# A two-layer transformer kernel: keys of the memory projected before the compression, weights loaded in 1 MB halves

## What is computed

```python
h = h + hier_moe(n2, ...)                                   # 32 experts, w1, w3, w2 of 2 MB each
gate = sigmoid(rms_norm(h, g_ple) @ w_ple_gate + b_ple_gate)
h = h + gate * (p @ w_ple_proj)
hn = rms_norm(h, norm_mix)
gq, gk, gv, gr, glr, nq, kc, vc, ks, vs, kw, vw, ng = split(hn @ w_in)
o_gla = gla_mixer(gq, gk, gv, gr, glr, ...)                 # decays by a running sum of log gates
o_nsa = nsa_mixer(nq, kc, vc, ...)                          # k_cmp = gelu(blocks(kc) @ w1) @ w2, the same for v
h = h + concat(o_gla, o_nsa) @ w_out
memn = rms_norm(mem, norm_mem)                              # 256 x 1024
k, v = memn @ wk, memn @ wv                                 # keys and values of the memory
h = h + cross_attn(rms_norm(h), k, v)
```

## Time and profile before

| what | us |
|---|---|
| median of 3 runs | 2139.96 (2139.68 to 2143.33) |
| the profiled execution, its own time | 2138.03 |
| its span, first to last instruction | 2136.3 |
| PE matmul busy | 1963.4 (92%) |
| DVE busy | 1377.9 (64%) |
| ACT busy | 1167.0 (55%) |
| HBM read | 415.36 MB, 195 GB/s over the span |

### The profile page before, as it was taken

The page is one execution under the profiler, slowest core; times in us unless marked ns, Lnnn a source line. Parts: engine busy times, 40 slices in busy tenths (PEclk is TensorE's granted clock), DMA queues, the critical chain, the costliest instruction groups (busy, mean ns, idle before and its releaser), DMA issues. The chain is left out here.

```text
span 2136.3 us, 29176 instructions
## 1 busy us (share of the span) xinstructions
PE 1963.4 (92%) x11497; PEld 1683.1 (79%) x11497; DVE 1377.9 (64%) x1828; ACT 1167.0 (55%) x1849; POOL 6.0 (0%) x27
## 2 busy tenths in 40 slices
PE   6998759999999998878889898999999999999997
PEld 5987448888888887367767577999999998888886
DVE  3552259999989898123543223999878896666665
ACT  3442149988989896124333242444477774545544
POOL 1000000000000000000000000000000000000000
PEclk9999869999999999989689999999999999999999
DMA  8433317999899899334012301455444444556664
GB/s 312 161 119 131 118 79 320 372 370 360 366 371 376 347 378 390 123 154 158 20 40 79 118 11 50 167 181 176 158 158 129 132 136 165 191 196 193 192 196 139
DMA packets 66175, 418.32 MB, mean 196 GB/s; under 512 B 12076, under 2 KB 14575, under 8 KB 49145
## 3 DMA queue, kind: packets, MB, share of 16 engines
q1 hardware_dynamic: 55728, 406.97, 51.3%
q10 hardware_dynamic: 10312, 9.48, 1.5%
HBM read 415.36 MB, written 1.06 MB: 195 GB/s over the span
## 5 line engine op out<-in xcount | busy, mean ns | idle before, releaser
L2113 DVE TENSOR_TENSOR slot_lo<-arena,w_hi 128x2048 fp32r<-128x2048 f32 x192 | 433.6, 2286 | 50.0 <-ACT w_hi L1579 49.9
L2468 DVE TENSOR_TENSOR tab_lo<-arena,tab_hi 128x1024 fp32r<-128x1024 f32 x256 | 312.4, 1224 | 122.9 <-ACT tab_hi L1884 120.8
L1579 ACT CAST w_hi<-arena 128x2048 fp32r<-128x2048 f32 x192 | 363.1, 1915 | 25.3 <-PE bank L1039 11.5
L1884 ACT CAST tab_hi<-arena 128x1024 fp32r<-128x1024 f32 x256 | 267.6, 1046 | 0.2
L1435 PE MATMUL bank<-x_hi,tab_lo 128*128 128x256 f32 x1024 | 145.0, 285 | 7.9 <-DVE tab_lo L2468 7.9
L1435 PE MATMUL bank<-x_hi,tab_hi 128*128 128x256 f32 x1024 | 148.5, 288 | 2.0 <-ACT tab_hi L1884 2.0
L1035 PE MATMUL bank<-w_hi,gathP 128*128 128x512 f32 x512 | 142.5, 401 | 7.6 <-ACT gathP L1584 5.4
L1918 ACT CAST e_hi<-arena 128x256 fp32r<-128x256 f32 x128 | 52.0, 407 | 175.1 <-PE bank L1468 174.4
L1435 PE MATMUL bank<-nT_lo,tab_hi 128*128 128x256 f32 x1024 | 143.0, 281 | 0.0
L1039 PE MATMUL bank<-slot_lo,gathP 128*128 128x512 f32 x512 | 140.3, 396 | 0.5 <-DVE slot_lo L2113 0.5
L1891 ACT ACTIVATE arena<-bank 128x256 f32<-128x256 f32 (+16 forms) x128 | 43.9, 343 | 175.1 <-PE bank L1435 175.0
(11 more groups left out here) (407 smaller groups left out, 3240.5 us busy)
## 6 DMA issues: line engine op xcount, KB each, us to landing
arena<-in_w_dram SPq DMA_DIRECT2D x96, 2048.0 KB, 12.0
arena<-in_peer_down_dram SPq DMA_DIRECT2D x128, 512.0 KB, 3.3
arena<-in_peer_up_dram SPq DMA_DIRECT2D x128, 512.0 KB, 4.3
arena<-in_packed_later_dram SPq DMA_DIRECT2D x18, 2048.0 KB, 7.8
arena<-in_packed_first_dram SPq DMA_DIRECT2D x14, 2048.0 KB, 8.7
arena<-in_packed_later_dram SPq DMA_DIRECT2D x1, 1632.0 KB, 15.7
arena<-in_packed_later_dram SPq DMA_DIRECT2D x1, 1536.0 KB, 12.3
h<-in_x_dram ACTq DMA_DIRECT2D x1, 1024.0 KB, 4.9
```

The costliest lines, as they stand in the source:

```text
L1579: nc.scalar.copy(hi_of(e, g), portion_of(slot, e, g)).then_inc(S("w_hi"), 1)
L1884: nc.scalar.copy(tab_hi[n % HI][:, :], tab[n % PR]).then_inc(S("table_hi"), 1)
L2113: nc.vector.tensor_tensor(portion_of(slot_lo, e, g), portion_of(slot, e, g), hi_of(e, g).bitcast(F32), ALU.subtract).then_inc(S("w_lo"), 1)
L2468: nc.vector.tensor_tensor(tab_lo[n % PR][:, :], tab[n % PR], tab_hi[n % HI][:, :].bitcast(F32), ALU.subtract).then_inc(S("table_lo"), 1)
```

## The change

The parts are these.
- Loads: every slot is loaded by two DMAs of 1 MB (column halves) with a semaphore each. In the expert stage a half is loaded when its own portion is used up, and ACT's cast of a portion waits for its half alone; `w2` is laid out anew so that its halves are column halves too. Elsewhere both halves wait for the same event as before, and users wait for both. PEER's table loads keep their size and use the slot semaphores.
- Between the layers: ACT reads gate tiles 0 and 1, squares the memory (`mem_sq`), casts the two portions, reads gate tile 2, does the first half's norm statistics, reads gate tile 3, does the second half's. PE sums the memory's squares behind the gate tiles; DVE normalises the memory behind `norm_cols`.
- Projection: the logarithm and running sum stand beside the fourth to sixth portion; the positions are turned behind `glr`; `dup` stands ahead of `nq`. The phase ends behind the projection and behind the compression are gone; DVE starts its GLA preparation when `nq` is done.
- The eight key tiles stand behind `nq`, whole, in banks 4 to 7. Then `gla_far`, the hidden layer of the compression, `gla_near`, the compression's outputs, `gla_blocks`, the output products, the compressed scores, the transposes.
- The sparse loop: only the eight value tiles are left, half a tile (8 matmul instructions) in each of steps 3 to 18.
- Two extra semaphores of the router are folded into others.

```diff
-    for name in ("w1", "w3", "w2"):
+    for name in ("w1", "w3"):
         arrays[name] = np.stack([rows_on_partitions(e) for e in inputs[name][0]])
+    arrays["w2"] = np.stack([np.concatenate([rows_on_partitions(e[:, 512 * x:512 * x + 512]) for x in range(2)], axis=1)
+                             for e in inputs["w2"][0]])
     arrays["peer_down_2"] = inputs["peer_down_2"].reshape(NKEYS, P, KT, P).transpose(0, 3, 2, 1).reshape(NKEYS, P, D)
...
-            if g < 4:
-                return v[:, 2048 * (g % 2):2048 * (g % 2) + 2048].rearrange("p (k n) -> p k n", n=512)
-            return v[:, :].rearrange("p (k n) -> p k n", n=D)[:, :, 512 * (g % 2):512 * (g % 2) + 512]
+            return v[:, 2048 * (g % 2):2048 * (g % 2) + 2048].rearrange("p (k n) -> p k n", n=512)
...
-        mem_sq = scratch(B0, KT, T)
-        xkT = scratch(B0, KT, T)
+        mem_sq = scratch(B0 + 4608, KT, T)
+        xkT = small[:, :].rearrange("p (k t) -> p k t", t=T)
...
-        landed = [S(f"slot_landed_{r}") for r in range(RING)]
+        landed = [[S(f"landed_{r}_{x}") for x in range(2)] for r in range(RING)]
...
+            for x in range(2):
+                half_ready(eng, n, x, i)
+
+        def half_ready(eng, n, x, i=0):
+
+            eng.wait_ge(landed[n % RING][x], i * 16 + 16 * (n // RING + 1))
...
+            b = tile_bank(pe, ("mem_sums", 0))
+            pe.wait_ge(S("mem_squared"), 1)
+            for k in range(KT):
+                mm = nc.tensor.matmul(b[:, 0:T], lhsT=ones[:, :], rhs=mem_sq[:, k, :], start=k == 0, stop=k == KT - 1)
+            mm.then_inc(S("tile_done"), 1)
...
-            for b, m in ((0, 0), (1, 1), (4, 2), (5, 3)):
+
+            pe.wait_ge(S("pos_ready"), 1)
+            pe.wait_ge(S("tile_read"), tile_no["kv", 3] + 1)
+            for m in range(4):
                 for g in range(2):
...
-                    mm = nc.tensor.matmul(bank[b][:, T * g:T * g + T], lhsT=sel_dup[:, g, :], rhs=kvT[:, m, :],
+                    mm = nc.tensor.matmul(bank[m][:, T * g:T * g + T], lhsT=sel_dup[:, g, :], rhs=kvT[:, m, :],
                                           start=True, stop=True)
                 mm.then_inc(S("dup_done"), 1)
...
+            layer_T(pe, "mix2", "nq", ports[6:8], 0)
...
+            def mem_part(c, b, ks):
+                at = LATE_AT + 9 + c // 4
+                slot_ready(pe, at)
+                wv = slot_view(at, KT, 512)
+                for k in ks:
+                    if c < KT:
+                        lhsT, rhs = wv[:, k, P * (c % 4):P * (c % 4) + P], memT[:, k, :]
+                    else:
+                        t, x = c % 4 // 2, c % 2
+                        lhsT, rhs = memT[:, k, P * t:P * t + P], wv[:, k, T * x:T * x + T]
+                    mm = nc.tensor.matmul(b[:, 0:T], lhsT=lhsT, rhs=rhs, start=k == 0, stop=k == KT - 1)
+                if ks[-1] == KT - 1:
+                    mm.then_inc(S("tile_done"), 1)
+                    if c % 4 == 3:
+                        spent(at)
+
+            pe.wait_ge(S("mem_normed"), 1)
+            for c in range(KT):
+                mem_part(c, tile_bank(pe, ("mem", c)), range(KT))
...
+            pe.wait_ge(S("cmp_in_ready"), 2)
             gla_far()
+            cmp_hidden()
             gla_near()
+            cmp_out()
             gla_blocks(1)
             gla_blocks(2)
             pe.wait_ge(S("gla_far_copied"), 2)
...
                 mm.then_inc(S("gla_out"), 1)
+            cmp_score()
...
+            def value_half(c, half):
+                if half == 0:
+                    n = tile_no["mem", c] = len(tile_no)
+                    if c >= KT + 2:
+                        pe.wait_ge(S("tile_read"), n - 1)
+                mem_part(c, bank[6 + c % 2], range(4 * half, 4 * half + 4))
...
-                if 0 <= i - MEM_FROM < MEM_TILES:
-                    mem_tile(i - MEM_FROM)
+                if 0 <= i - MEM_FROM < MEM_HALVES:
+                    value_half(KT + (i - MEM_FROM) // 2, (i - MEM_FROM) % 2)
...
-                slot_ready(act, MOE_AT + 3 * e + g // 2)
+                half_ready(act, MOE_AT + 3 * e + g // 2, g % 2)
...
+            gate(0, 0)
+            gate(0, 1)
+            act.wait_ge(S("mem_in"), 16)
+            nc.scalar.activation(mem_sq[:, :, :], memT[:, :, :], ACT.Square).then_inc(S("mem_squared"), 1)
             layer_first(act, "mix2")
-            norm_act(act, chain, "mix2", h, ple_added)
+            gate(1, 0)
+            norm_act_rows(act, chain, "mix2", h, 0, ple_added)
+            gate(1, 1)
+            norm_act_rows(act, chain, "mix2", h, 1, ple_added)
+            b = tile_in(act, ("mem_sums", 0))
+            nc.scalar.activation(mem_rms, b[:, 0:T], ACT.Sqrt, bias=eps[:, 0:1], scale=1.0 / D).then_inc(S("tile_read"), 1)
+            act.wait_ge(S("tile_read"), tile_no["mem_sums", 0] + 1)
+            act.sem_inc(S("mem_rooted"), 1)
...
+                if q == 2:
+                    act.wait_ge(S("tile_read"), tile_no[("loga", 1)] + 1)
+                    chain(nc.scalar.activation(log_tmp, loga[:, :, :], ACT.Abs))
+                    chain(nc.scalar.activation(log_tmp, log_tmp, ACT.Exp, scale=-1.0))
+                    nc.scalar.activation(log_tmp, log_tmp, ACT.Ln, bias=1.0).then_inc(S("log_part"), 1)
+                if q == 6:
+                    act.wait_ge(S("dup_done"), 4)
+                    for s in range(2):
+                        nc.scalar.copy(dupT[:, 2 * s:2 * s + 2, :].rearrange("p g t -> p (g t)"), bank[2 + s][:, :])
...
-            act.wait_ge(S("cmp_w1_in"), 32)
-            phase_end(act, "act")
...
-            nc.scalar.copy(posT[:, :, :].rearrange("p s i -> p (s i)"), bank[6][:, 0:2 * SUB]).then_inc(S("pos_ready"), 1)
             k_exp(0)
-            act.wait_ge(S("dup_done"), 4)
-            for s in range(2):
-                nc.scalar.copy(dupT[:, 2 * s:2 * s + 2, :].rearrange("p g t -> p (g t)"), bank[4 + s][:, :])
+            read_mem(0)
             act.wait_ge(S("diag_diff"), 1)
             nc.scalar.activation(diag[:, :, :, :], diag[:, :, :, :], ACT.Exp).then_inc(S("diag_exp"), 1)
+            read_mem(1)
             q_exp(1)
             k_exp(1)
+            read_mem(2)
             q_exp(2)
+            for c in range(3, KT):
+                read_mem(c)
             act.wait_ge(S("cmp_hidden"), 1)
-            nc.scalar.activation(cmp_h[:, :, :], bank[2][:, 0:64].rearrange("p (s n) -> p s n", s=2)[:, :, 0:2 * N_CMP],
...
+
+            dve.wait_ge(S("mem_rooted"), 1)
+            chain(nc.vector.reciprocal(mem_rms, mem_rms))
+            for k in range(KT):
+                ins = nc.vector.scalar_tensor_tensor(out=memT[:, k, :], in0=memT[:, k, :], scalar=col("norm_mem_2", k),
+                                                     in1=mem_rms, op0=ALU.mult, op1=ALU.mult)
+            ins.then_inc(S("mem_normed"), 1)
+
+            def decays(q, x):
+                if (q, x) != (3, 0):
+                    return
+                dve.wait_ge(S("log_part"), 1)
+                chain(nc.vector.tensor_scalar(loga[:, :, :], loga[:, :, :], 0.0, None, ALU.min))
+                chain(nc.vector.tensor_tensor(loga[:, :, :], loga[:, :, :], log_tmp, ALU.subtract))
+                chain(nc.vector.tensor_scalar(loga[:, :, :], loga[:, :, :], 0.5 / 16.0, None, ALU.mult))
+                for c in range(2):
+                    ins = nc.vector.tensor_tensor_scan(bcum[:, c, :], loga[:, c, :], loga[:, c, :], 0.0, ALU.add, ALU.add)
+                chain(ins)
+                cg = nsa_gate[:, 0, :].rearrange("p (a b) -> p a b", b=3)[:, :, 0]
+                nc.vector.tensor_scalar(cg, cg, late_row[:, 0:1], None, ALU.mult)
+
+            layer_dve(dve, "mix2", ("glr", 0), decays)
+            dve.wait_ge(S("tile_done"), tile_no["nq", 3] + 1)
 
...
+                width = src.shape[1] // 2
+                for x in range(2):
+                    if n >= RING:
+                        m = n - RING
+                        if m in spent_at:
+                            sp.wait_ge(S("tile_done"), spent_at[m])
+                        else:
+                            e, kind = (m - MOE_AT) // 3, (m - MOE_AT) % 3
+                            wait_portion(sp, e, 2 * kind + x)
+                    cols = slice(width * x, width * x + width)
+                    sp.dma_start(slot[n % RING][:, cols], src[:, cols]).then_inc(landed[n % RING][x], 16)
...
+                    for x in range(2):
+                        if j % 3 < 2:
+                            sp.wait_ge(S("w13_used"), i * 8 + (4 * (j // 3 - 2) + 2 * (j % 3) + x + 1))
+                        else:
+                            sp.wait_ge(S("w2_used"), i * 4 + (2 * (j // 3 - 2) + x + 1))
+                        cols = slice(2048 * x, 2048 * x + 2048)
+                        sp.dma_start(slot[(MOE_AT + j) % RING][:, cols], src[:, cols]).then_inc(
+                            landed[(MOE_AT + j) % RING][x], 16)
             for m, pieces in enumerate(later):
```

(30 more changed lines are left out.)

197 lines of the change are left out of this document (70 added, 127 removed).

## The result

The changed kernel takes 2086.30 us (median of 4 runs, 2085.36 to 2090.44) against 2140.34 of the kernel before on the same chip: ratio 0.9749, 95% interval 0.9732 to 0.9766, a gain of 54.0 us where 45.3 were forecast. 2086.3 lies inside the range of 2079 to 2111. The profiled execution took 2087.17 us, 50.9 less than the one of before (2138.03).

The account below looks back on a forecast made before the run. PE was taken as the bound, busy in 92% of 2136.3 us. Terms -7.2 - 2.0 + 3.5 + 4.3 - 10.4 - 27.5 - 6.0 = -45.3 us took 2139.96 to 2094.7; range 2079 to 2111.

Parts of the forecast that it names:

- step 3: End of `nq` to the loop: key tiles fill PE's wait, thin matmuls lose the clock; 73.4 us against 69.1, +4.3 us.
- Between the layers: Last gate tile to projection: casts and first-half statistics hide under gate products, projection starts at 911.8; -7.2 us.
- The clock's share: Projection's start: with less idle time ahead it need not begin at the lower clock; -2 us, between 0 and -2.1.
- `dup`: Projection: its 16 instructions, moved ahead of `nq`, take 3.44 us at full clock; +3.5 us.
- Start of the loop: Loop's start to first memory tile: about 7 us remain of 17.4; -10.4 us.
- The loop: Sparse loop: eight of 16 tiles leave it while PE stays the bound; -27.5 us, second-half steps 4.66 us.
- The rival of a loop bound by its chain: Sparse loop: steps can't go under perhaps 4.8 us because of DVE and ACT stages; +13 us, 2107.7; chance 0.15.
- Halves in the expert stage: Expert stage: ACT's 8.4 us of weight waits should go, most having reached PE; -6 us, between 0 and -8.4.
- the one with full clock behind the keys: Hidden layer through output products: PE's idle time drops the clock, so it stays full; 13.2 us more gain, 2081.5; chance 0.17.
- The stage bound by DMA: Expert stage: 8 KB rows move only at 377 GB/s, an expert takes 19.2 us instead of 17.0; 2170.7; chance 0.04.

Follow-up runs that it names:

- e5_order_back: The changed kernel with ACT's order between the layers put back, casts and both gates ahead of the row statistics; 2099.81 us.
- e9_spread_late: The changed kernel with the hidden layer's 64 thin products behind the last four key tiles, sixteen behind each; 2082.94 us.
- e11_bare_loop: The changed kernel with all 16 value halves in step 0 of the sparse loop and none later; 2100.78 us.
- e3_both: The changed kernel, still issuing transfers in halves, but ACT's cast of an expert's portion waits for both halves of its slot; 2100.06 us.
- e2_wholes: The changed kernel with its transfers put back: one transfer of a whole slot and one wait for it; 2103.99 us.
- e6_spread: The changed kernel with the hidden layer's 64 thin products spread among the eight key tiles, eight behind each; 2098.53 us.
- e1_halves: The kernel before with only the change's transfers: slots loaded in halves, ACT's cast waiting for its own half; 2125.26 us.
- e4_first_whole: The changed kernel with the first six slots, the first projection's weights, loaded whole and everything later in halves; 2084.29 us.

## Why the prediction was right

The sign, the range and all large terms but one held; the time came 8.4 us under the forecast. The sum is nearer than its terms, since their errors partly cancel: the expert stage gained 7.2 us more than its term and step 3 was 3.6 better, while the time ahead of the stage, the projection and the loop's start came out 3.3, 2.0 and 1.3 worse. By its own steps:

1. **Between the layers**: -7.5 against -7.2 (919.09 less the forecast's 911.8 is 7.3), and e5_order_back confirms the order as the cause. The clock's share failed: the float32 projections take 30.6 us after 30.3, at 0.92 after 0.93. Less idle time ahead did not save the first microseconds from the lower clock: 0 in place of -2.
2. **`dup`**: 3.61 us, forecast 3.44, seen whole in the projection's +3.5.
3. **Keys instead of waiting**: 69.8 us against 73.4. DVE's preparation starts at 990.76, 0.9 us behind the end of `nq`; the eight tiles took 27.79 (27.5). The hidden layer was mis-sized, 10.6 against 12.5: the high clock held for 3.6 us of it, not two. `gla_near` took 7.6, not 8.5, and here the working was wrong and not only the size: the sum gave it 1.6 us for the clock (8.5 against 6.9), and e9_spread_late has 7.44 at full clock throughout. The reading behind the step, that thin products lose the clock although PE is busy, agrees with three runs (behind the keys here, lost; among dense tiles in e9_spread_late, kept; in e11_bare_loop, lost for 30.7 us), though the last also regained it without a dense tile.
4. **Start of the loop**: 8.3 us against 7. All of it ran at half clock, which the estimate left out.
5. **The loop**: -28.5 against -27.5, with steps of 3.35 to 3.57 us in the first half. In the second they took 3.4 to 4.65, the four longest 4.43 to 4.65 where 4.66 were forecast. The rival of a loop bound by its chain did not come about here: PE is busy 62.79 of 63.00 us. In the bare loop, at half clock, PE was busy throughout as well; what its first half would take at full clock is not known.
6. **Halves in the expert stage**: the step that was off, -13.2 against -6, beyond its bound of -8.4. I took ACT's waits for weights as the ceiling. But the issue in halves alone shortens the stage by 6.3 us (e3_both against e2_wholes), with ACT's cast still waiting for the whole slot, and the cast's own half brings 6.5 more. PE's idle time fell by 8.3 us, about the bound; the other 4.9 are busy time for the same matmuls, close to half of the 10.2 us at half clock before, and the clock was in no term of this step. Pieces at half clock stand inside the stage in all three kernels in which ACT waits for whole slots (10.2 us before, 3.4 in e2_wholes, 6.8 in e3_both) and in none of the other eleven. What they cost is open: e2_wholes, with 3.4 us of them, takes 524.6 us, the kernel before, with 10.2, takes 524.9.

Of the rivals, the one with full clock behind the keys gave 2081.5, nearer to the result than the forecast by luck, since its mechanism is refuted: the half clock stands where the forecast had it. The rule of the Trainium skill weighed there ("TensorE: Matmul & The Clock Gate", the table of rules at its end), which ties drops to idle gaps, does not cover e11_bare_loop's second row. The stage bound by DMA did not appear: 8 KB rows moved 372 GB/s on average over it at a share of 0.96, so a queue of 1 MB transfers stays above the 341 GB/s that the Trainium skill gives for a single one ("DMA: Bandwidth & Descriptors", Bandwidth, Measured).

Left open: why the half clock ahead of PEER lasts 3.4 us in five traces, 13.7 in five and 17.1 in four with the same code, and what the idle microseconds ahead of the projection have to do with its slow start.

## What to carry to other kernels

Work that depends on nothing late is best kept as dense filler and put where PE waits or runs thin products: here the same eight tiles were worth 23 us more there than in a loop that had no gaps. When a stage repeats a pipeline near its limit, the waits seen for transfers are no ceiling for what earlier and smaller ones bring: here 13.2 us where the waits were 8.4. And read each edit's effect in its own stretch, since 4 us and more moved elsewhere in the same code.

## What the runs showed of the hardware that was not expected

- PE busy in 30.70 of 30.70 us ran at half clock (e11_bare_loop). Among dense tiles thin products ran at full clock: sixteen behind each of the last four of eight tiles (e9_spread_late, 35.8 us in all), or eight behind each (e6_spread, from 1008 us on).
- Pieces of half clock stood in the expert stage in the three kernels in which ACT waited for whole slots, at most 2.4 us each time, and in none of eleven others, though PE is busy in 506.9 of 524.9 us there.
- The 32 products of `gla_near` (64x256) took 7.59 us with 3.2 us of them at half clock and 7.44 at full (e9_spread_late). Half of 3.2 us would be 1.6; 0.15 is what the clock cost them at most.
- Splitting the weight transfers of one queue into halves let another queue's transfer land earlier, after 17.3 us (e1_halves) in place of 27.4 (the kernel before) or 26.7 (e4_first_whole).
